# q and k scale in a hybrid decoder step: Sqrt on ScalarE and a reciprocal on VectorE in place of Ln and Exp

## The reference, cut to what matters

```
def _l2norm(x):
    xf = x.astype(jnp.float32)
    return xf * lax.rsqrt(jnp.sum(xf * xf, axis=-1, keepdims=True) + L2_EPS)
...
    qkv, conv_new = _causal_conv(qkv, conv_buf, conv_w)      # silu inside
    q, k, v = jnp.split(qkv, 3, axis=-1)
    q = _l2norm(q.reshape(shp))
    k = _l2norm(k.reshape(shp))
...
    q = q * (dk ** -0.5)                                     # in _gated_delta
```

## Time and profile before

| | us |
|---|---|
| median of 3 runs | 1689.77 (1689.38 to 1692.36) |
| the profiled execution | 1691.89 |
| its span, first to last instruction | 1690.2 |
| TensorE busy | 1515.9 (90%) |
| VectorE busy | 737.2 (44%) |
| ScalarE busy | 396.8 (23%) |

### The profile page before, as it was taken

One profiled execution on the slowest core, in us unless ns is written; L12 is line 12 of the kernel. 1 busy time (PEld: TensorE's weight loads), 2 busy tenths in 40 slices (PEclk: granted clock), 3 DMA queues, 4 the chain that ended last, 5 costly groups with the idle time before them and its releaser, 6 DMA issues.

```text
span 1690.2 us, 16119 instructions
## 1 busy us (share of the span) xinstructions
PE 1515.9 (90%) x6083; PEld 947.4 (56%) x6083; DVE 737.2 (44%) x1295; ACT 396.8 (23%) x639; POOL 207.9 (12%) x224
## 2 busy tenths in 40 slices
PE   8999999989998999699999599999939999999960
PEld 6676666546656656356989466555424444444420
DVE  4667865023253332885785333245432221112118
ACT  3211101116575483231211500011111111111103
POOL 0000100000000000354277000000110000000014
PEclk9999999999999999789899799999969999999985
DMA  5274864414311113224101712132378999999937
GB/s 160 78 126 125 247 206 106 144 52 116 88 52 39 35 31 110 63 63 143 58 1 29 305 57 74 65 114 111 122 268 290 362 374 373 363 368 376 365 126 282
DMA packets 226021, 273.25 MB, mean 162 GB/s; under 512 B 62420, under 2 KB 158024, under 8 KB 225680
## 3 DMA queue, kind: packets, MB, share of 16 engines
q1 hardware_dynamic: 198388, 203.54, 38.3%
q10 hardware_dynamic: 18140, 34.48, 5.4%
q0 software_dynamic: 9408, 34.08, 5.2%
HBM read 188.83 MB, written 83.24 MB: 161 GB/s over the span
## 4 chain that ended last, share of the span: by engine, by line
PE 75%; DVE 8%; ACT 7%; issue 4%; DMA 2%; POOL 2%; ACTq 0%; POOLq 0%; DVEq 0%
PE P L677 23%; PE P L1117 12%; PE P L1068 7%; PE P L1026 7%; PE P L1101 6%; PE P L834 2%; PE P L858 2%; POOL arena L587 2%; PE P L1088 2%; DVE arena L1407 1%; PE P L703 1%; PE P L809 1%; DMA arena<-y_d,arena 1%; DMA x_d<-arena 1%; PE P L692 1%
## 5 line engine op out<-in xcount | busy, mean ns | idle before, releaser
L677 PE MATMUL P<-arena 128*128 128x352 f32 (+1 forms) x1728 | 537.6, 467 | 0.1
L677 PEld LDWEIGHTS P<-arena 128*128 128x128 f32 (+1 forms) x1728 | 325.5, 192 | 186.6 <-issue 27.6
L1117 PE MATMUL P<-arena 128*128 128x512 f32 x512 | 227.1, 597 | 0.8 <-ACT arena L2146 0.8
L1117 PEld LDWEIGHTS P<-arena 128*128 128x128 f32 x512 | 95.6, 192 | 109.5 <-issue 109.5
L1068 PE MATMUL P<-arena 128*128 128x512 f32 (+1 forms) x288 | 128.9, 597 | 1.9 <-DVEq L1565 1.9
L1026 PE MATMUL P<-arena 128*128 128x352 f32 x384 | 115.8, 465 | 8.6 <-DVE arena L1551 8.6
L1709 DVE COPY arena<-P 128x512 f32<-128x512 f32 x32 | 22.1, 691 | 220.3 <-PE P L1088 220.3
L1101 PE MATMUL P<-arena 128*128 128x512 f32 x256 | 115.3, 593 | 0.9 <-DVE arena L1743 0.9
L1026 PEld LDWEIGHTS P<-arena 128*128 128x128 f32 x384 | 74.0, 193 | 50.9 <-issue 11.1
L587 POOL TENSOR_TENSOR arena<-arena,N 64x256 f32<-64x256 f32 x96 | 79.3, 826 | 50.0 <-ACT arena L2081 26.9
L1068 PEld LDWEIGHTS P<-arena 128*128 128x128 f32 (+1 forms) x288 | 50.2, 181 | 62.3 <-issue 59.7
(11 more groups left out here) (393 smaller groups left out, 1877.0 us busy)
## 6 DMA issues: line engine op xcount, KB each, us to landing
arena<-in_w_expert_up_dram SPq DMA_DIRECT2D x32, 2048.0 KB, 13.6
arena<-in_w_expert_down_dram SPq DMA_DIRECT2D x32, 1024.0 KB, 7.9
arena<-in_w_in_dram SPq DMA_DIRECT2D x36, 512.0 KB, 4.2
x_d<-zero SPq DMA_DIRECT2D x4, 4096.0 KB, 20.1
arena<-x_d POOLq DMA_DIRECT2D x32, 512.0 KB, 6.1
y_d<-arena ACTq DMA_DIRECT2D x32, 512.0 KB, 7.9
gate_d<-arena ACTq DMA_DIRECT2D x16, 528.0 KB, 4.4
arena<-gate_d SPq DMA_DIRECT2D x16, 528.0 KB, 4.5
```

The costliest lines, as they stand in the source:

```text
L677: m = pe.matmul(P[0:p, b + j, 0:TBK], w[:, k, 0:p], hT[:, k, TBK * j:TBK * j + TBK], start=f, stop=l)
L1117: m = pe.matmul(P[:, i % 2, :], xgT[i % 2][:, k, :], WU[i % NWE][:, k, :], start=k == 0, stop=k == KD - 1)
```

## The change

ScalarE writes the square root of the sum plus epsilon into `RN` with one Sqrt, which raises `s_ssr`. Its second instruction and the wait between the two are gone. VectorE waits for `s_ssr` instead of `s_rn`, takes the reciprocal of `RN` in place (a new instruction over 128 x 1056), and then scales as before. This happens for each of the 8 q and k jobs.

```
@@ VectorE, step n, job m = n - 1
-                    dve.wait_ge(s_rn, QK_COUNT(m))
+                    dve.wait_ge(s_ssr, QK_COUNT(m))
+                    link(dve.reciprocal(RN, RN))
                     o = QT[:, hp] if kind == "q" else KST
                     dve.scalar_tensor_tensor(o, o, DH ** -0.5 if kind == "q" else 1.0, RN, ALU.mult,
                                              ALU.mult).then_inc(s_qk, 1)
@@ ScalarE, the same job
-                        act.activation(blocks3(RN), P[:, b:b + NBK, 0:TBK], ACT.Ln, bias=cst[:, 0:1]).then_inc(s_ssr, 1)
-                        act.wait_ge(s_ssr, QK_COUNT(m))
-                        act.activation(RN, RN, ACT.Exp, scale=-0.5).then_inc(s_rn, 1)
+                        act.activation(blocks3(RN), P[:, b:b + NBK, 0:TBK], ACT.Sqrt, bias=cst[:, 0:1]).then_inc(s_ssr, 1)
```

## The result

| | us |
|---|---|
| kernel before, median of 6 runs beside it | 1692.78 (1689.38 to 1694.35) |
| changed kernel, median of 6 runs | 1715.67 (1713.7 to 1723.42) |
| ratio, 95% interval | 1.0153 (1.0133 to 1.0172) |
| span of the profiled execution | 1713.9 (before: 1690.2) |

A forecast was written before the change was run, and what follows sets the result against it. TensorE, 90% busy, bounds the kernel, with next to no cover where it waits for the edited chain. Chain 16.0, table load 0.1 and clock 7 us make 23 us: 1715, or 1713 us as the runs' median; range 1704 to 1727.

The forecast's parts named there:

- Which path counts: At each q and k job, delaying L2001 delays TensorE's L843 equally; waits there grow from 6.4 to some 22 us.
- The price of the reciprocal: VectorE's new reciprocal over 1056 elements takes 6.7 us, from the slope between 128 elements (942 ns) and one (164 ns).
- The rival of eight element times: VectorE's reciprocal costs 8.9 us per tile, 18 us more on the chain: 1731 us; chance 0.06.
- that of a streaming reciprocal: VectorE's reciprocal runs like an ordinary operation, 1.26 us, so the kernel gets faster: 1682 us; chance 0.05.
- The point of balance: Reciprocal length on VectorE at which the new chain equals the old: 4.6 to 4.8 us; below it no loss.
- The gain on the other side: With a cheap reciprocal, ScalarE's earlier copies let TensorE take back 4 x 1.9 = 7.6 us at the q jobs.
- The chain's 16.0 us: From Ln's end to L2001 or L1996: 2.07 us later per q job, 1.93 per k job, over four pairs.
- the fourth rival: Slips are absorbed downstream, for instance in TensorE's 4.44 us stall at 533; chance 0.05.
- The clock's 7 us: Longer TensorE stalls at L843 lower its clock; three in four followed by a fall, between 0 and 20 us.
- short fall: A 3.4 us stretch of TensorE at clock 0.51, costing at most 1.7 us, or 0.6 at a q job.
- The rival without falls: TensorE's clock does not fall, only the 16.1 us of the chain remain: 1706 us; chance 0.26.
- The added table load: Table load ahead of L2032 pushes L2010 from 508.44 to 509.7; TensorE's L858 waits 0.1 us.

The follow-up runs named there:

- the run with 4.65 us: Kernel without the reciprocal, plus a reciprocal over 720 of the 1056 columns: 1693.19 us, ratio 1.0011 to the kernel before.
- The filled kernels: Changed kernel with four extra matmuls of 352 columns in TensorE's wait at each q and k job, measured twice: 1706.34 and 1708.29 us.

## Why the prediction was right

**Which path counts.** As put: L843 waits for L2001, L2001 for the scaling, and VectorE's reciprocal stands in front. Forecast was about 22 us of wait at L843, measured 23.4 and 25.3 in two profiles. Part of the excess goes with the clock: of the stalls at k jobs in the first profile, those whose q job was followed by a fall are 3.45 and 3.46 us, the other two 2.95 and 3.02.

**The price of the reciprocal.** Taken at 6.69 us from a row with 128 elements, measured 6.75. The rival of eight element times (8.9 us) and that of a streaming reciprocal (1.26 us) are both excluded by the new row itself. The point of balance, worked out at 4.6 to 4.8 us, was hit by the run with 4.65 us, which came out at the kernel before.

**The gain on the other side.** Put at 7.6 us at most; the kernel without the reciprocal measured 7.

**The chain's 16.0 us.** The filled kernels stand 16 and 18 us over the kernel before, with the clock at 1.00 at all eight jobs. The q job q0 took 8.24 us from Sqrt's end to L2002, and k0 8.23 us to L1997, where the sum said 8.13. Nothing was absorbed in the stall that waits for L1437, the fourth rival: it is 4.4 us in both kernels.

**The clock's 7 us.** This was the guess of the sum, three stalls in four with a short fall, between 0 and 20 us. The filling gives it as 8 us. The size agrees, and part of that is luck. The sum had six short falls of eight; in one execution four fell, in another all eight, and there those behind k jobs were twice as long. In the first a third of the added time at half clock stood behind other waits. The sum's premise that stalls of up to 1.1 us leave the clock alone held for the stretch of the trace it was read from and not for every execution. The rival without falls (1706 us) is what the filled kernel shows, 1706 and 1708 us.

**The added table load** ahead of the Exp of the decay matrix: TensorE's wait for its bank was 0.48 us, against the 0.1 of the sum. The rows of the changed kernel:

```profile
521.42 1.86 PEld L858 LDWEIGHTS P<-arena 128*128 128x128 f32 x16 [0.48 <-ACT arena L2011]
521.42 2.00 PE L858 MATMUL P<-arena 128*128 128x64 f32 x16
```

It stood at 510.48 before, without a wait. This is too small to matter.

Against the 1713 us forecast stand 1715.67 and 1716.37 us. What the sum had too low is 0.1 us per job in the chain and about 1 us of the clock. That is less than the spread of the measurement: the medians lie 22.9 us apart on one occasion and 27.0 us on the other.

## What to carry to other kernels

Before moving work to an engine that is half idle, ask what is queued behind the place where it goes: here 54 us on an engine with 950 us of idle time cost the kernel 33 us, because each piece stood between TensorE and the instruction it waits for. Price an unusual operation by its slope between two sizes in the trace, not by its element count; then work out at what price the edit turns from gain to loss, and cut the operation to that size to test it. A stall that grows may cost twice, once as waiting and again as slower work behind it; the second part differs from execution to execution, so one profile is not enough to size it.

## What the runs showed of the hardware

VectorE's fp32 reciprocal takes 6.25 to 6.27 ns per element per partition between 128, 720 and 1056 elements (942, 4652 and 6752 ns), where a scalar_tensor_tensor takes 1.04. The 942 ns row has 16 partitions, the others 128.

Stalls of TensorE of 2.8 to 3.5 us were followed by the 1.2 GHz level for 3.4 or 6.8 us in some executions and not in others, while stalls of 0.45 to 0.98 us at the same line, L843, left it at 2.4 GHz in the kernel before. Waits of 0.84 to 1.15 us at L884 in the v jobs were followed by 3.4 us at 1.2 GHz in 9 of 14 profiles, 14 times in all, and most such waits by none. Where the stalls were longer, none was without a fall: with the reciprocal added to Ln and Exp, eight stalls of 5.2 to 5.9 us each had one of 6.8 us, and with two reciprocals eight stalls of 8.4 to 10.2 us each had one of 10.2 us. These falls begin before TensorE resumes, at 417.7 us where it resumes at 419.43 in the first of them:

```profile
419.43 0.40 PE L843 MATMUL P<-shift_id,VS 128*32 128x128 f32 x1 [5.24 <-ACT VS L2002]
```
```profile
417.70:424.40 6.70, 4.97 (x10) 2.97 (x11) 5.90 (x8) 2.32 (x4) 0.00 (x0) 0.50 0.01 2
```

Keeping TensorE at useless matmuls through the eight stalls (2.0 to 3.5 us) made the changed kernel 8 us faster than leaving it idle.
